# Gate and up projections as Strassen block products in an fp32 encoder layer

## The reference

```python
def swiglu(x, wg, wu, wd):
    return (jax.nn.silu(x @ wg) * (x @ wu)) @ wd
...
    h = x + 0.5 * swiglu(rmsnorm(x, g_ffn1), w1g, w1u, w1d)
    ...                      # two kinds of attention, one output projection
    h = h + 0.5 * swiglu(rmsnorm(h, g_ffn2), w2g, w2u, w2d)
```

## Time and profile before

| | |
|---|---|
| median of three runs | 1196.58 us (1196.19 to 1197.70) |
| the profiled execution, its span | 1196.7 us |
| PE, DVE, ACT, POOL busy in it | 1136.6, 514.5, 354.2, 102.7 us |
| feed-forward 1, attention, feed-forward 2 | about 0 to 440, 440 to 760, 760 to 1197 us |

### The profile page before, as it was taken

One profiled execution on the slowest core, in us unless ns is written; L12 is line 12 of the kernel. 1 busy time (PEld: TensorE's weight loads), 2 busy tenths in 40 slices (PEclk: granted clock), 3 DMA queues, 4 the chain that ended last, 5 costly groups with the idle time before them and its releaser, 6 DMA issues.

```text
span 1196.7 us, 19887 instructions
## 1 busy us (share of the span) xinstructions
PE 1136.6 (95%) x8218; PEld 1102.3 (92%) x8218; DVE 514.5 (43%) x763; ACT 354.2 (30%) x549; POOL 102.7 (9%) x93
## 2 busy tenths in 40 slices
PE   7999999999999999878898859999999999999996
PEld 7999999999999999767777649999999999999996
DVE  5543443443322223656677643354444444422214
ACT  5322222222222223233334533332222222212112
POOL 4000000000010110412122102100000000000001
PEclk8999999999999999988999869999999999999998
DMA  5222222223222231300120202222222222332202
GB/s 203 89 76 82 88 74 84 88 77 115 89 82 72 90 142 53 124 13 3 43 73 34 67 1 88 74 87 83 75 88 85 72 88 88 102 98 73 78 19 79
DMA packets 27515, 93.84 MB, mean 78 GB/s; under 512 B 3472, under 2 KB 6544, under 8 KB 27344
## 3 DMA queue, kind: packets, MB, share of 16 engines
q1 hardware_dynamic: 27472, 93.23, 23.7%
HBM read 88.24 MB, written 4.98 MB: 78 GB/s over the span
## 4 chain that ended last, share of the span: by engine, by line
PE 85%; DVE 9%; ACT 3%; issue 1%; DMA 0%; POOL 0%; DVEq 0%; SPq 0%; ACTq 0%; POOLq 0%
PE acc L462 79%; PE acc L592 3%; PE acc L687 1%; DVE w_lo L1072 1%; DVE st L1251 1%; DVE st L1244 1%; DVE u_lo L1077 1%; ACT probs L964 1%; ACT probs L954 1%; ACT w_hi L787 1%; DVE probs L1285 1%; DVE turned L1223 1%; PE acc L700 0%; DMA raw<-in_w1gu 0%; PE acc L657 0%
## 5 line engine op out<-in xcount | busy, mean ns | idle before, releaser
L1072 DVE TENSOR_TENSOR w_lo<-raw,w_hi 128x1024 fp32r<-128x1024 f32 (+2 forms) x145 | 195.3, 1347 | 532.0 <-ACT w_hi L787 532.0
L462 PE MATMUL acc<-u_hi,w_hi 128*128 128x288 f32 x1616 | 356.8, 303 | 6.7 <-DVE w_lo L1072 4.9
L462 PE MATMUL acc<-u_lo,w_hi 128*128 128x288 f32 x1616 | 349.6, 298 | 0.0
L462 PE MATMUL acc<-u_hi,w_lo 128*128 128x288 f32 x1616 | 349.3, 298 | 0.0
L787 ACT ACTIVATE w_hi<-raw 128x1024 fp32r<-128x1024 f32 (+2 forms) x145 | 164.7, 1136 | 407.0 <-PE acc L462 392.5
L462 PEld LDWEIGHTS acc<-u_hi,w_hi 128*128 128x128 f32 x1616 | 263.0, 191 | 18.6 <-issue 12.1
L462 PEld LDWEIGHTS acc<-u_lo,w_hi 128*128 128x128 f32 x1616 | 263.4, 191 | 0.0
L462 PEld LDWEIGHTS acc<-u_hi,w_lo 128*128 128x128 f32 x1616 | 263.4, 191 | 0.0
L462 PE MATMUL acc<-h_hi,w_hi 128*128 128x288 f32 x704 | 155.0, 297 | 0.0
L462 PE MATMUL acc<-h_hi,w_lo 128*128 128x288 f32 x704 | 154.9, 297 | 0.0
L462 PE MATMUL acc<-h_lo,w_hi 128*128 128x288 f32 x704 | 154.7, 297 | 0.0
(11 more groups left out here) (174 smaller groups left out, 875.5 us busy)
## 6 DMA issues: line engine op xcount, KB each, us to landing
raw<-in_w1gu SPq DMA_DIRECT2D x44, 512.0 KB, 3.7
raw<-in_w2gu SPq DMA_DIRECT2D x44, 512.0 KB, 3.7
raw<-in_w1d SPq DMA_DIRECT2D x16, 704.0 KB, 4.0
raw<-in_w2d SPq DMA_DIRECT2D x16, 704.0 KB, 4.1
raw<-in_w_qk SPq DMA_DIRECT2D x13, 512.0 KB, 4.6
raw<-in_w_out SPq DMA_DIRECT2D x8, 512.0 KB, 3.8
raw<-in_w_v SPq DMA_DIRECT2D x4, 640.0 KB, 3.9
res<-in_x SPq DMA_DIRECT2D x4, 576.0 KB, 7.0
```

The costliest lines, as they stand in the source:

```text
L462: m = nc.tensor.matmul(acc[:, bank + t, 0:HALF], w_part[slot][:, col:col + P], x_part[:, k, t * HALF:(t + 1) * HALF], start=first and n == ...
L1072: nc.vector.tensor_tensor(w_lo[w_static % SPLIT_SLOTS][:, 0:width], raw[w_static % RAW_SLOTS][:, 0:width], w_hi[w_static % SPLIT_SLOTS][:, ...
```

## The change

The 22 hidden tiles are run in two chunks of 11, each followed by its own half of the down projection (8 tiles d with 11 k steps, and one more addition to `res` for each d, so 16 a block instead of 8). Tiles f = 0 to 3 (`PLAIN`) are made as before. For f = 4 to 21 (18 in each feed-forward block), gate and up together are a 2 x 2 block product: the weights are a11, a12, a21, a22 of 512 columns each (two halves of the input width, for gate and for up), the activations are 2 halves of the input width by 2 token halves. `pair_products` makes it by the Winograd form of Strassen's scheme with 7 products (`PARTS`) of 4 k steps and three matmuls each, 84 matmuls of 288 columns, in the order P1, P5, P6, P2, P7, P3, P4. P1, P6, P7 and P4 gather in one PSUM bank, and ACT copies partial sums out between them (`snap`).

What it needs beside: seven combinations of the activations, `c_hi` and `c_lo`, made once for each feed-forward block from `res`, the gain and `rrow` (`combine` and `combine_lo` on DVE, `comb_hi` on ACT), one k step of the four in each plain tile; and four sums of weight blocks for each f, slots 0 to 3 of `w_sum`, which lies in the memory of `comb`. POOL makes slots 0 and 2 (`raw_weight_sums`), DVE slots 1 and 3 (`weight_sums`). ACT and DVE split the sums, a11 with a12, and a22 (`hi_sums`, `hi_a1`, `hi_a22`, `lo_sums`, `lo_a1`, `lo_a22`; a group is split when its low part is made, and `split_ready` counts groups). `w_hi` and `w_lo` have one place for each of the seven products, and no second set.

Moved or resized: `norm_sums` now stands in up of f = 0, at k = 2; on ACT the squares of the first norm all come ahead of the split of block (f = 1, gate); raw slots are three of 1 MB; loops are written out; the last down tile has 11 k steps for each token half, with the sums of the first half at k = 6 of the second (before: 22 k steps and k = 4); `turned` and `rope_x` of the attention share the memory of `ssq` and `sq`.

The core of the diff: first PE, then ACT from `hi_sums` on, then DVE from `weight_sums` on, and last POOL.

```diff
+            def wait_pair_banks(ffn, f, n):
+                if n not in (P1, P5, P2):
+                    return
+                if f in (PLAIN, PLAIN + 1):
+                    pe.wait_ge(u_out, KF * ffn + f - 1)
+                elif f == CHUNK_F + 1:
+                    pe.wait_ge(half_added, KD * ffn + KD)
+                else:
+                    former = f - 1 if f == CHUNK_F else f - 2
+                    if n == P1:
+                        pe.wait_ge(c21_out, pairs_before(ffn, former) + 1)
+                    else:
+                        pe.wait_ge(g_out, KF * ffn + former + 1)
...
+            def pair_products(ffn, f):
+                group = GROUP[("st", ffn, f)]
+                snaps = 4 * pairs_before(ffn, f)
+                for n, (banks, c) in enumerate(PRODUCTS):
+                    pe.wait_ge(split_ready, group + {P1: 2, P5: 1, P6: 1, P2: 2, P7: 3, P3: 3, P4: 4}[n])
+                    wait_pair_banks(ffn, f, n)
+                    if n in (P6, P7, P3, P4):
+                        pe.wait_ge(snapped, snaps + {P6: 1, P3: 2, P7: 3, P4: 4}[n])
+                    for k in range(KH):
+                        if f == PLAIN:
+                            pe.wait_ge(c_ready, KH * ffn + k + 1)
+                        col = n * PART + k * P
+                        for e, (w_part, x_part) in enumerate(((w_hi, c_hi), (w_hi, c_lo), (w_lo, c_hi))):
+                            m = nc.tensor.matmul(acc[:, banks[side(f)], 0:HALF], w_part[:, col:col + P],
+                                                 x_part[:, k, c, :], start=n in (P1, P5, P2) and k == 0 and e == 0,
+                                                 stop=k == KH - 1 and e == 2, skip_group_check=True)
+                    m.then_inc(block_used, 1)
...
+            def hi_sums(ffn, f, half):
+                act.wait_ge(sum_ready, 2 * pairs_before(ffn, f) + 1 + half)
+                act.wait_ge(raw_sums, 2 * pairs_before(ffn, f) + 1 + half)
+                first = (P5, P7)[half]
+                if f == CHUNK_F or f == PLAIN:
+                    act.wait_ge(block_used, sums_free(ffn, f)[half])
+                else:
+                    act.wait_ge(block_used, UNIT[("st", ffn, f - 1)] + (P6, P3)[half] + 1)
+                nc.scalar.activation(w_hi[:, first * PART:(first + 2) * PART].rearrange("p (s n) -> p s n", s=2),
+                                     w_sum[:, 2 * half:2 * half + 2, :], ACT.Copy).then_inc(hi_ready, 1)
...
+            def comb_hi(ffn_no, j):
+                act.wait_ge(comb_ready, KH * ffn_no + j + 1)
+                nc.scalar.activation(c_hi[:, j, 0, :], comb[:, 0, :], ACT.Copy)
+                nc.scalar.activation(c_hi[:, j, 1:PARTS, :], comb[:, 2:PARTS + 1, :], ACT.Copy).then_inc(chi_ready, 1)
...
+            def plain_gate_up(ffn_no, f):
+                if f + 1 < PLAIN:
+                    hi_block(("gu", ffn_no, f + 1, 0))
+                if f == 0:
+                    rms(NORMS_BEFORE[ffn_no], NORM_BANK)
+                silu(ffn_no, f)
+                if ffn_no and f == 0:
+                    act.wait_ge(k_stored[B_HEADS - 1], 16)
+                    act.wait_ge(bs_stored, 16)
+                comb_hi(ffn_no, f)
+                if f + 1 < PLAIN:
+                    hi_block(("gu", ffn_no, f + 1, 1))
+                    hidden_hi(ffn_no, f)
+                else:
+                    hi_sums(ffn_no, PLAIN, 0)
+                    hi_a1(ffn_no, PLAIN)
...
+            def pair_period(ffn_no, f):
+                first, last = first_of_chunk(f), last_of_chunk(f)
+                if first:
+                    hi_sums(ffn_no, f, 1)
+                else:
+                    take_c21(ffn_no, f - 1)
+                hi_a22(ffn_no, f)
+                if not first:
+                    silu(ffn_no, f - 1)
+                act.wait_ge(u_out, KF * ffn_no + f)
+                snap(snap_g[:, f % 2, 0, :], ffn_no, f, P1)
+                snap(snap_u[:, 1, :], ffn_no, f, P5)
+                snap(snap_g[:, f % 2, 1, :], ffn_no, f, P6)
+                if last:
+                    hi_block(("dn", ffn_no, f // CHUNK_F, 0))
+                else:
+                    hi_sums(ffn_no, f + 1, 0)
+                if f != CHUNK_F:
+                    hidden_hi(ffn_no, f - 1)
+                if not last:
+                    hi_a1(ffn_no, f + 1)
+                snap(snap_u[:, 0, :], ffn_no, f, P7)
+                if not last:
+                    hi_sums(ffn_no, f + 1, 1)
+                else:
+                    take_c21(ffn_no, f)
+                    silu(ffn_no, f)
+                    hidden_hi(ffn_no, f)
+                    hi_block(("dn", ffn_no, f // CHUNK_F, 1))
...
+            def weight_sums(ffn, f):
+                key = ("st", ffn, f)
+                made = 2 * pairs_before(ffn, f)
+                raw_now = raw[LOAD[key] % RAW_SLOTS]
+                a11, a12 = raw_now[:, 0:PART], raw_now[:, PART:2 * PART]
+                s1, s2, s4 = w_sum[:, 0, :], w_sum[:, 1, :], w_sum[:, 3, :]
+                dve.wait_ge(raw_sums, made + 1)
+                nc.vector.tensor_tensor(s2, s1, a11, ALU.subtract).then_inc(sum_ready, 1)
+                dve.wait_ge(sum_ready, made + 1)
+                nc.vector.tensor_tensor(s4, a12, s2, ALU.subtract).then_inc(sum_ready, 1)
...
+            def combine(ffn_no, j):
+                if ffn_no or j:
+                    dve.wait_ge(c_ready, KH * ffn_no + j)
+                for e in range(2):
+                    m = nc.vector.scalar_tensor_tensor(out=comb[:, 2 * e:2 * e + 2, :].rearrange("p c n -> p (c n)"),
+                                                       in0=res[:, j + KH * e, :],
+                                                       scalar=gains[:, 2 * ffn_no, j + KH * e:j + KH * e + 1],
+                                                       in1=rrow[:], op0=ALU.mult, op1=ALU.mult)
+                then(m)
+                then(nc.vector.tensor_tensor(comb[:, 4:7:2, :], comb[:, 1:4:2, :], comb[:, 0:2, :], ALU.subtract))
+                then(nc.vector.tensor_tensor(comb[:, 5, :], comb[:, 3, :], comb[:, 4, :], ALU.subtract))
+                nc.vector.tensor_tensor(comb[:, 7, :], comb[:, 2, :], comb[:, 5, :], ALU.subtract).then_inc(comb_ready, 1)
...
+            def combine_lo(ffn_no, j):
+                dve.wait_ge(chi_ready, KH * ffn_no + j + 1)
+                dve.wait_ge(comb_ready, KH * ffn_no + j + 1)
+                nc.vector.tensor_tensor(c_lo[:, j, 0, :], comb[:, 0, :], c_hi[:, j, 0, :].bitcast(FP32), ALU.subtract)
+                nc.vector.tensor_tensor(c_lo[:, j, 1:PARTS, :], comb[:, 2:PARTS + 1, :],
+                                        c_hi[:, j, 1:PARTS, :].bitcast(FP32), ALU.subtract).then_inc(c_ready, 1)
...
+            def plain_gate_up(ffn_no, f):
+                if f + 1 < PLAIN:
+                    lo_block(("gu", ffn_no, f + 1, 0))
+                if f == 0:
+                    dve.wait_ge(rms_done, NORMS_BEFORE[ffn_no] + 1)
+                    nc.vector.reciprocal(rrow[:], rrow[:]).then_inc(r_ready, 1)
+                    dve.wait_ge(r_ready, NORMS_BEFORE[ffn_no] + 1)
+                gate_out(ffn_no, f)
+                combine(ffn_no, f)
+                if f + 1 < PLAIN:
+                    up_out(ffn_no, f)
+                    lo_block(("gu", ffn_no, f + 1, 1))
...
+            def take_c1(ffn_no, f):
+                dve.wait_ge(block_used, UNIT[("st", ffn_no, f)] + P3 + 1)
+                dve.wait_ge(h_full, KF * ffn_no + f)
+                bank = B_BANK[side(f)]
+                nc.vector.tensor_tensor(halves(gate[:, :]), acc[:, bank:bank + 2, 0:HALF], snap_g[:, f % 2],
+                                        ALU.add).then_inc(g_out, 1)
...
+            def pair_period(ffn_no, f):
+                first, last = first_of_chunk(f), last_of_chunk(f)
+                if f == PLAIN:
+                    up_out(ffn_no, f - 1)
+                if first:
+                    lo_sums(ffn_no, f, 1)
+                lo_a22(ffn_no, f)
+                if not last:
+                    weight_sums(ffn_no, f + 1)
+                if f != CHUNK_F:
+                    hidden(ffn_no, f - 1)
+                if last:
+                    lo_block(("dn", ffn_no, f // CHUNK_F, 0))
+                else:
+                    lo_sums(ffn_no, f + 1, 0)
+                if f != CHUNK_F:
+                    hidden_lo(ffn_no, f - 1)
+                if not last:
+                    lo_a1(ffn_no, f + 1)
+                take_c22(ffn_no, f)
+                take_c1(ffn_no, f)
+                if not last:
+                    lo_sums(ffn_no, f + 1, 1)
+                else:
...
+            def raw_weight_sums(ffn):
+                for f in range(PLAIN, KF):
+                    key = ("st", ffn, f)
+                    gp.wait_ge(raw_in[LOAD[key] % RAW_SLOTS], 16 * (LOAD[key] // RAW_SLOTS + 1))
+                    if f == PLAIN:
+                        gp.wait_ge(c_ready, KH * (ffn + 1))
+                    else:
```

(72 more changed lines are left out.)

632 lines of the change are left out of this document (334 added, 298 removed).

## The result

The changed kernel takes 1184.25 us (median of 4 runs, 1183.18 to 1186.32), the kernel before 1197.14 (4 runs, 1196.19 to 1198.61). The ratio is 0.9893, 95% interval 0.9877 to 0.9908, so it is faster by 1.1%. The forecast was 1182.0. The profiled execution has a span of 1184.5 us, before 1196.7, a difference of 12.2.

The account below looks back on a forecast made before the run. The feed-forward stages were taken as bound by PE's matmul count alone. 1196.7 - 57.6 saved + 15.0 + 19.3 (passages) + 4.0 (clock) + 4.5 (end) = 1181.9, taken as 1182 us; range 1168 to 1200.

Parts of the forecast that it names:

- attention stage: Between the two feed-forward blocks; the prediction's sum has no term for it.
- the first pair's period: First pair after each 12 us PE idle: half clock costs 1.7 us, taken as 2.0 for each of two.
- the tail: End of the program: second token half has 33 matmuls instead of 66, DVE's cover is gone, 4.5 us lost.
- 432 matmuls: 12 of 96 matmuls go in each of 36 pairs, at 0.1333 us each: 57.6 us saved.
- feed-forward 1 with its clock: Start of the first block's pairs: P1 at 85.3 instead of 66.0, loss 19.3 us, plus 2.0 for the clock.
- feed-forward 2, clock, tail: Second block's passage to the pairs loses 15.0 us, its clock 2.0, the program's end 4.5.
- pair boundaries: Between pairs: a period of 11.2 us, P1 of the next pair ready 0.45 us early, so no wait.
- contention: POOL's four last additions before `norm_sums` in feed-forward 1: a little contention puts their end at 25.9.
- The turns: Plain tiles, `gate_out` to `gate_out`, through DVE and ACT: 13.2, 13.2 and 12.0 us; PE's turn is 12.8.
- The last leg: From `gate_out` of f = 3 to the first pair's P1, nothing ready ahead: 14.8 us.
- Both idles: PE idle ahead of each block's first pair, about 12 us each, ended by DVE's low parts.
- One meeting with POOL in the chain: Pair boundary: one POOL addition holds DVE about 1.2 us; none leaves P1 1.6 us early, two 0.75 late.

Follow-up runs that it names:

- experiments 3 to 5: Changed kernel with ScalarE splitting the next up block before `comb_hi` (1178.43 us), with five plain tiles instead of four (1171.86 us), and with both edits (1158.31 us).
- experiment 2: Changed kernel with the low part of a11 and a12 made twice in each pair: 1205.76 us, ratio 1.0063 to the kernel before.
- experiment 1: Changed kernel with VectorE making all four weight sums and POOL none: 1183.78 us, ratio 0.9883 to the kernel before.
- 6: Changed kernel with five plain tiles, ScalarE's split before `comb_hi`, and all four weight sums on VectorE: 1157.87 us, ratio 0.9657 to the kernel before.
- 7: Changed kernel with five plain tiles, ScalarE's split before `comb_hi`, and feed-forward 1's norm products at k = 7 instead of 2: 1157.19 us, ratio 0.9658 to the kernel before.

## Why the prediction was right

The mechanism was as predicted: all of the saving comes from the matmul count, and most of it is given back where the pairs begin. The terms, from events that both traces have. Up to the wait for `q_diag` in the attention stage (493.20 in the earlier trace rows, 486.63 after, rows below) lie 18 pairs, 28.8 us, and the shift is 6.57, so feed-forward 1 gave back 22.2. Up to `norm_sums` of feed-forward 2 (777.02 less the 8.0 of its new place, 765.04 after) the shift falls to 4.0. To the end it is 12.2, so feed-forward 2 and the tail gave back 28.8 - 8.2 = 20.6.

By place, the first pair starts 20.1 us later than f = 4 did (86.34 against 66.25) and in feed-forward 2 14.1 later (both against `norm_sums`), where 19.3 and 15.0 were predicted; the first pair's period is 1.5 and 1.7 us over 11.24 (2.0 each predicted); the tail cost 4.2 (4.5 predicted); the rest is 0.6 in each block.

| term | predicted | measured |
|---|---|---|
| 432 matmuls | -57.6 | -57.6 (432 gone, 11.23 a pair against 11.2) |
| feed-forward 1 with its clock | 19.3 + 2.0 | 22.2 |
| attention stage | 0 | 2.6 |
| feed-forward 2, clock, tail | 15.0 + 2.0 + 4.5 | 20.6 |
| pair boundaries | 0 | 0 |
| sum | -14.8 | -12.2 |

Without the attention stage the measured terms make -14.8, the predicted sum to the tenth. That is luck: feed-forward 1 gave back 0.9 us more than predicted, feed-forward 2 with the tail 0.9 less.

**Feed-forward 1.** `norm_sums` came at 27.04 instead of 26.4: the last of POOL's additions took 2.48, held by a low part of DVE that began at the same time.

```profile
22.96 1.40 POOL L1766 TENSOR_TENSOR ssq<-ssq,sq 128x576 f32<-128x576 f32 x1
24.51 2.48 POOL L1766 TENSOR_TENSOR ssq<-ssq,up 128x576 f32<-128x576 f32 x1
...
24.51 1.22 DVE L1286 TENSOR_TENSOR w_lo<-raw,w_hi 128x1024 fp32r<-128x1024 f32 x1 [4.53 <-ACT w_hi L949]
```

They answer to the earlier trace rows; the prediction allows 0.4 for contention, from 19.25 + 4 x 1.57 = 25.5 to 25.9. From there to the first `gate_out` it took 6.89 instead of the 5.73 of the earlier trace rows, with PE at half clock (the four matmuls of the norm took 2.29 against 1.13); in feed-forward 2 it took 5.73 exactly. The turns were 12.84, 12.82 and 11.70 (predicted 13.2, 13.2, 12.0). The last leg took 15.05 from `gate_out` at 71.29 to PE (14.8 predicted), in the order that the prediction gives:

```profile
77.30 0.46 DVE L1397 TENSOR_TENSOR c_lo<-comb,c_hi 128x288 fp32r<-128x288 f32 x1 [2.04 <-ACT c_hi L1027]
77.68 1.95 DVE L1398 TENSOR_TENSOR c_lo<-comb,c_hi 128x1728 fp32r<-128x1728 f32 x1
81.07 1.73 DVE L1324 TENSOR_TENSOR comb<-comb,raw 128x512 f32<-128x512 f32 x1 [1.44 <-POOL comb L1754]
...
85.07 1.22 DVE L1286 TENSOR_TENSOR w_lo<-raw,w_hi 128x1024 fp32r<-128x1024 f32 x1
```

P1 stood 59.3 us behind `norm_sums` (58.9 predicted), 58.2 in feed-forward 2. Both idles were 11.83 (12 predicted). That they are made of the late steps of DVE and ScalarE is shown by experiments 3 to 5, in which they fall to 8.7, 3.0 and 0.

**The boundary.** The prediction had P1 ready 0.45 us early; the rows give 0.65 (132.75 - 132.05, less 0.05 from DVE to PE), experiment 2 about 0.5. One meeting with POOL in the chain was right.

**The tail.** PE waited 4.71 at L727, where it waited 0.54 before; from PE's last weight product to the end it is 4.2 us longer than before. DVE's sums of the first and the second half stand without a gap (the row at 1173.40 answers to the one at 1185.53 in the earlier trace rows):

```profile
1169.74 3.73 DVE L1711 SCALAR_TENSOR_TENSOR res<-res,gains,rrow 128x288 f32<-128x288 f32 x6
1173.40 0.44 DVE L1704 SCALAR_TENSOR_TENSOR res<-acc,res 128x288 f32<-128x288 f32 x1
```

**The term that was missed** is the attention stage, at 0 in the prediction; its work is the same before and after, only two of its buffers lie elsewhere. After the same wait the half clock lasted longer; windows of 3 us from there, in which the row ends with granted clock, DMA share and GB/s:

```profile
486.40:489.40 3.00, 2.77 (x13) 2.12 (x14) 0.84 (x4) 0.00 (x0) 0.18 (x1) 0.50 1.05 257
489.40:492.40 3.00, 3.00 (x14) 3.00 (x14) 1.48 (x4) 1.42 (x7) 0.00 (x0) 0.51 0.90 351
492.40:495.40 3.00, 3.00 (x23) 2.47 (x22) 1.34 (x3) 0.62 (x4) 0.00 (x0) 1.00 0.05 22
495.40:498.40 3.00, 1.52 (x11) 1.04 (x9) 2.86 (x13) 2.03 (x10) 0.00 (x0) 1.00 0.00 0
498.40:501.40 3.00, 2.46 (x11) 2.13 (x12) 2.25 (x4) 1.43 (x2) 2.70 (x2) 0.62 0.01 3
```

The same stretch of the kernel before:

```profile
493.00:496.00 3.00, 2.80 (x13) 2.15 (x14) 0.88 (x4) 0.00 (x0) 0.15 (x1) 0.50 0.96 268
496.00:499.00 3.00, 3.00 (x23) 2.65 (x22) 1.46 (x4) 1.44 (x7) 0.00 (x0) 0.93 1.02 403
...
505.00:508.00 3.00, 3.00 (x24) 2.83 (x23) 2.60 (x4) 0.30 (x1) 2.84 (x3) 1.00 0.14 20
```

PE did 14 matmuls in the second window where before it did 23, and fell to half clock once more at 499. The whole 2.6 us are lost in the first 100 matmuls behind the wait; from there on the two traces keep the same distance.

The change doesn't always bring this. From that wait to `norm_sums` of feed-forward 2 the stage took 275.8 us before (to their new place) and 278.4 after. The experiments run the same attention code: 275.7 in experiment 1, 276.8 in 6, and 277.5 to 278.8 in 2, 3, 4, 5 and 7. So it is not a fixed price of the change: with the change and without it the stage can take the same time, and what differs is the granted clock. The two shortest are the runs without POOL's weight sums; with one trace of each that may be chance. Why the half clock lasts 3 us in one execution and 6 in another the traces don't tell, and no run here was made to tell it.

## What to carry to other kernels

When an algorithm takes work off the bounding engine, look first at where it starts: its preparation is a serial chain over the other engines, and here it ate 34 of 57.6 us (20.1 and 14.1) while no boundary of the steady state waited. Such a chain is paid for by work that is ready anyway (one more plain tile) and by the order of the queues that it passes through; together these won 26 us more, twice the change's own gain. And an operation given to GpSimd is not free for VectorE: count what its additions add to the instructions beside them before counting what they take off.
